# One TensorE order and one branch of a four-block transformer kernel: merge products exchanged, rotation buffer, value turn and logits moved

## The reference, cut to what matters

```python
# block 1, per layer
merge_g = sigmoid(merge_r @ w_merge_up).reshape(b, s, 4, 1024)
for n in range(4):
    yb = branches[n] * silu(gate_z[:, :, n])
    merged = merged + merge_g[:, :, n] * (yb @ w_branch[n])
out = merged @ w_out

# block 2, per layer, branch A
q = axial_rope(rmsnorm(q_a, qn_a)); k = axial_rope(rmsnorm(k_a, kn_a))
p = softmax(q @ k.T * scale);  o_a = (p @ v) * silu(g_a)
```

## Time and profile before

| | |
|---|---|
| median of 3 runs | 1513.04 us (1512.2 to 1513.24) |
| profiled execution, its own time | 1514.28 us |
| its span | 1512.5 us |
| TensorE busy | 1418.9 us (94% of the span) |
| VectorE busy | 854.7 us (57%) |
| ScalarE busy | 729.5 us (48%) |
| GpSimd busy | 384.2 us (25%) |

### The profile page before, as it was taken

The page is one execution under the profiler, slowest core; times in us unless marked ns, Lnnn a source line. Parts: engine busy times, 40 slices in busy tenths (PEclk is TensorE's granted clock), DMA queues, the critical chain, the costliest instruction groups (busy, mean ns, idle before and its releaser), DMA issues.

```text
span 1512.5 us, 21589 instructions
## 1 busy us (share of the span) xinstructions
PE 1418.9 (94%) x8202; PEld 1101.7 (73%) x8202; DVE 854.7 (57%) x1553; ACT 729.5 (48%) x1557; POOL 384.2 (25%) x273
## 2 busy tenths in 40 slices
PE   7999999999989999999988889997999989988997
PEld 6767677778987677787778856665778856665776
DVE  3655436456662653455577665457656474457655
ACT  3555446555244554555554544435444544445443
POOL 2232122345131322123553111311112112310111
PEclk9999999999999999999999999998999999998999
DMA  6413451126242221112265413511323422511311
GB/s 225 112 30 88 109 136 43 51 68 227 87 154 61 53 84 57 56 46 63 91 216 162 118 52 63 118 57 49 97 65 94 116 70 55 92 60 46 101 61 57
DMA packets 195373, 135.76 MB, mean 90 GB/s; under 512 B 91590, under 2 KB 185414, under 8 KB 195270
## 3 DMA queue, kind: packets, MB, share of 16 engines
q1 hardware_dynamic: 191494, 120.22, 29.0%
q10 hardware_dynamic: 3776, 14.16, 2.5%
HBM read 122.03 MB, written 12.32 MB: 89 GB/s over the span
## 4 chain that ended last, share of the span: by engine, by line
PE 74%; DVE 12%; ACT 7%; issue 3%; DMA 2%; POOL 1%; SPq 1%; ACTq 0%; DVEq 0%; POOLq 0%
PE pb L1477 19%; PE pb L1479 17%; PE pb L1478 17%; PE pb L1560 6%; PE pb L1499 6%; PE pb L1538 5%; ACT prob L1616 2%; ACT tmp L1616 2%; ACT wh L1635 1%; DVE wl L1983 1%; DVE xl L1990 1%; DMA wr<-w_out 1%; DVE prob L2235 1%; PE pb L1522 1%; PE pb L1510 1%
## 5 line engine op out<-in xcount | busy, mean ns | idle before, releaser
L2376 POOL TENSOR_TENSOR wl<-wr,wh 128x512 fp32r<-128x512 f32 x178 | 254.2, 1428 | 857.6 <-ACT wh L1635 853.6
L1477 PE MATMUL pb<-xh,wl 128*128 128x512 f32 (+1 forms) x880 | 356.1, 405 | 11.4 <-DVE xl L1990 8.5
L1479 PE MATMUL pb<-xh,wh 128*128 128x512 f32 (+1 forms) x880 | 327.7, 372 | 0.0
L1478 PE MATMUL pb<-xl,wh 128*128 128x512 f32 (+1 forms) x880 | 327.6, 372 | 0.0
L1983 DVE TENSOR_TENSOR wl<-wr,wh 128x512 fp32r<-128x512 f32 x208 | 169.5, 816 | 183.5 <-ACT wh L1635 183.2
L1635 ACT CAST wh<-wr 128x512 fp32r<-128x512 f32 (+1 forms) x386 | 218.9, 604 | 38.0 <-PE pb L1479 17.1
L1477 PEld LDWEIGHTS pb<-xh,wl 128*128 128x128 f32 x880 | 169.2, 192 | 82.3 <-issue 47.0
L1479 PEld LDWEIGHTS pb<-xh,wh 128*128 128x128 f32 x880 | 168.7, 192 | 29.9
L1478 PEld LDWEIGHTS pb<-xl,wh 128*128 128x128 f32 x880 | 169.6, 193 | 22.3 <-issue 3.6
L1477 PE MATMUL pb<-wh,xl 128*128 128x256 f32 x448 | 133.2, 297 | 16.5 <-DVE wl L1983 8.4
L1616 ACT ACTIVATE prob<-prob,small 128x512 f32<-128x512 f32 (+3 forms) x128 | 76.3, 597 | 138.6 <-DVE small L2198 138.5
(11 more groups left out here) (197 smaller groups left out, 2443.1 us busy)
## 6 DMA issues: line engine op xcount, KB each, us to landing
wr<-w_in SPq DMA_DIRECT2D x39, 1024.0 KB, 5.2
wr<-w_out SPq DMA_DIRECT2D x14, 1024.0 KB, 5.4
wr<-w_in SPq DMA_DIRECT2D x48, 256.0 KB, 4.6
wr<-w_branch SPq DMA_DIRECT2D x48, 128.0 KB, 2.3
x<-prob SPq DMA_DIRECT2D x12, 512.0 KB, 3.3
wr<-w_out SPq DMA_DIRECT2D x48, 128.0 KB, 3.0
wr<-w_mem_kv SPq DMA_DIRECT2D x4, 1024.0 KB, 5.5
prob<-x ACTq DMA_DIRECT2D x2, 2048.0 KB, 10.6
```

The source lines that it names most:

```text
L1477: e.matmul(ps, ll, rh, start=start, stop=False)
L1478: e.matmul(ps, lh, rl, start=False, stop=False)
L1479: t = e.matmul(ps, lh, rh, start=False, stop=stop)
L2376: t = e.tensor_tensor(wl[:, j % 2, c0:c1], wr[:, j % 2, c0:c1], wh[:, j % 2, c0:c1].bitcast(F32), ALU.subtract)
```

## The change

There are four edits. (1) In the first column tile of the merge, the first term's branch product is made ahead of its gate product. (2) In branch A the rotated part is written to `tmpz`, a scratch row, in place of a `TM` slot. (3) In branch A the values are turned later: not in `project`, but as a part of branch B's projection, behind its third fill step; for A, B and D the wait for the turned values goes from the logits to the product with the values. (4) In branch A, a block's logits come at least 5000 planned ns behind those of the block before.

```diff
+FRONTS = 5000
@@ attention
-        before, late = None, None
+        before, late, apart = None, None, 0
...
             for i in range(4):
+                if now() < apart:
+                    yield apart
                 es, mid, after = front(l, br, c, i, sm.get(c), rt)
                 ready = now() + EXPS.get(br, 4000)
+                if br == "A":
+                    apart = now() + FRONTS
                 yield 0
@@ merge_term
+        opening = m == 0 and first
+        if opening:
+            held = yield from gemm("br", w, c0, c0 + 128, ("y", l, n), (k0, k0 + 1))
         b = yield from gemm("up", w, c0, c0 + 128, ("mr", l), (k0 + 2,))
...
-        b = yield from gemm("br", w, c0, c0 + 128, ("y", l, n), (k0, k0 + 1))
+        b = held if opening else (yield from gemm("br", w, c0, c0 + 128, ("y", l, n), (k0, k0 + 1)))
@@ project, behind
-            b, t2 = GR[0].take(), TM.take()
+            b, t2 = GR[0].take(), None if br == "A" else TM.take()
             put("rope2", l=l, br=br, n=n, src=tm, b=b, tm=t2)
-            give(b, t2)
+            give(b, *[t2] * (br != "A"))
@@ project, end
-        b = GR[0].take()
-        put("vturn", l=l, br=br, b=b, tm=tm)
-        give(b, tm)
-        yield
+        def turned():
+            b = GR[0].take()
+            put("vturn", l=l, br=br, b=b, tm=tm)
+            give(b, tm)
+
+        if br == "A":
+            box["vturn"] = turned
+        else:
+            turned()
+            yield
+
+    def then_turned(fill, turned):
+        for n, x in enumerate(fill):
+            if n == 2:
+                turned()
+            yield x
@@ block 2
+            if br == "A":
+                fill = then_turned(fill, turned)
@@ heads_ready
             elif br in PAIRED:
                 w.wait_ge(v_fn, v_fn.at(("paired", l, br, 2)))
-                w.wait_ge(v_copy, v_copy.at(("vturn", l, br)))
@@ pv on TensorE
+                if br in PAIRED:
+                    w.wait_ge(v_copy, v_copy.at(("vturn", l, br)))
@@ rope2 on VectorE
-                src, t2 = tm(s["src"]), tm(s["tm"])
+                src, t2 = tm(s["src"]), tmpz[:, :] if br == "A" else tm(s["tm"])
...
+                if br == "A":
+                    w.wait_ge(v_fn, v_fn.at(("rotated", l, n - 1) if n else ("rms2", 2 + l, 3)))
```

More of the change, by code:

```diff
@@ L1104, in plan @@
         for n, br in enumerate("ABDC"):
-            u = box["u"]
+            u, turned = box["u"], box.get("vturn")
             box = {}
             fill = project(l, "ABDC"[n + 1], box) if br != "C" else out_partial(l, tail, box)
+            if br == "A":
+                fill = then_turned(fill, turned)
             if br == "B":
@@ L2284, in vector_program @@
                 w.wait_ge(aux, aux.at(b))
-                for g, v in s["tm"].free():
-                    w.wait_ge(g, v)
+                if br == "A":
+                    w.wait_ge(v_fn, v_fn.at(("rotated", l, n - 1) if n else ("rms2", 2 + l, 3)))
+                else:
+                    for g, v in s["tm"].free():
+                        w.wait_ge(g, v)
                 w.wait_ge(d_tab, d_tab.at((l, br)))
@@ L2294, in vector_program @@
                     w.wait_ge(heado, heado.at(("heado", l, "A", 1)))
-                ends = (s["tm"],) if br == "A" else (s["tm"], s["src"])
                 t = e.tensor_tensor(dst, src, t2, ALU.add)
-                t.then_inc(v_fn.sem, v_fn.mark(*([] if br == "A" else [("paired", l, br, n)]), ends=ends))
+                if br == "A":
+                    t.then_inc(v_fn.sem, v_fn.mark(("rotated", l, n)))
+                else:
+                    t.then_inc(v_fn.sem, v_fn.mark(("paired", l, br, n), ends=(s["tm"], s["src"])))
             elif k == "qnormed":
```

## The result

The changed kernel takes 1517.76 us (median of 11 runs, 1513.09 to 1519.53); the kernel before, in as many runs, 1513.04 (1512.1 to 1517.44). The ratio is 1.0022, with a 95% interval of 1.0012 to 1.0032: 1.8 to 4.8 us slower (the two medians lie 4.7 apart). The forecast was 1515.7 and slower by 2.7; its range holds the time, and the interval holds the 2.7. The profiled executions stand at spans of 1516.0 and 1512.5.

What follows compares the result with a forecast made beforehand. TensorE carries most of the chain, so time counts only where it idles. Openings 0, branch A 1.9 and 0, clock 2.0, behind the logits -1.2: 2.7 us more, 1515.7 as a median against 1513.04; range 1508.0 to 1519.5.

Steps and rivals of the forecast that it cites:

- Merge openings: Block 1's merge, both layers: TensorE's wait for the low half becomes 1.6 us for the tanh; 0.0 us each.
- The table load's price: Merge opening, ScalarE: load takes 1.28 us by its row; the skill's drain would end each opening 1.3 us later.
- Rival 3: Merge openings: the table load holds the tanh 1.28 us longer, 2.6 us on top, 1518.3; chance 0.03.
- Branch A, layer 0, up to the logits: Block 2: banks held behind VectorE's stretch bring logits at 892.2 against 890.95, one group left undone; 1.9 us lost.
- The wait of 1.4 for that bank: Branch A, layer 0: TensorE waits 1.4 us for VectorE's normalisation to free the squares' bank ahead of the value turn.
- Branch A, layer 1, up to the logits: Logits wait for the keys alone, 0.7 us earlier, with 0.69 left undone; 0.0, bounds 0.5 either way.
- The wait of 3.3 in one piece: Branch A, layer 1: TensorE stands about 3.3 us in one wait ahead of the logits.
- The clock: Branch A: 3.4 us at 0.50 behind long waits costs 1.7 us in layer 1, 0.3 in layer 0; 2.0 lost.
- Rival 2: Branch A, both layers: the lower clock lasts longer, as the 5.7 us seen elsewhere; 1519.3 us; chance 0.20.
- full clock throughout branch A: Sign that the forecast is wrong: no stretch at a clock of 0.5 in branch A.
- Behind the logits: Branch A: spacing removes waits of 1.36 and 0.25 us, new ones of 0.95 and 0.5 come; 0.6 gained per layer.
- Rival 1: Bubbles are filled: merges give 1.57 us each, spacing 1.6 each, no slow stretch; about -5 us, 1508; chance 0.22.

Runs made afterwards that it cites:

- e1: The kernel before with edit 1 alone (branch product ahead of gate product in the merge); ratio to the kernel before 1.0004.
- e6: The changed kernel with the table set that has the tanh chosen at branch fox's first logits, so no load in the merge opening; ratio to the kernel before 1.0007.
- e11: The kernel before with no table load in the merge opening and its order kept; ratio to the kernel before 0.9994.
- e5: The changed kernel with the third tile's rotation and squares in banks of the attention's ring; ratio to the kernel before 1.0010.
- e2: The kernel before with edit 2 alone (rotated part in the scratch row); ratio to the kernel before 1.0008.
- e7: e5's kernel with 3500 more planned ns of fill ahead of branch A's first logits; ratio to the kernel before 0.9929.
- e3: The kernel before with edit 4 alone (branch A's logits at a distance); ratio to the kernel before 0.9994.
- e9: The kernel before with only 3500 more planned ns of fill ahead of branch A's first logits; ratio to the kernel before 1.0003.
- e4: The changed kernel without edit 3 (values turned in A's own projection, waited for ahead of the logits); ratio to the kernel before 1.0018.
- e10: The changed kernel with e7's extra fill ahead of branch A's first logits but its own banks; ratio to the kernel before 0.9988.
- e12: e8's kernel with the distance between branch A's logits set to zero; ratio to the kernel before 0.9958.
- e8: e6 and e7 together; ratio to the kernel before 0.9904, median 1502.51 us.

## Why the prediction was right

The mechanism came as forecast: VectorE's stretch sets the logits of branch A, the table load sets the openings, and the loss is a longer wait with a slow stretch behind it. The sum was 2.7; the four places measure 2.59. That they agree so closely is luck, since the terms below miss by up to half a microsecond each way. The chances were less sure than the sum: 0.42 for a change within 0.2% and 0.36 for slower; the ratio came out at 0.22%.

- **Merge openings:** 0.0 each, measured +0.07 and +0.08. The tanh was to end at 281.95 and the branch product to start at 282.0; it is at 282.02 on the clock of before. e1 and e6 show the reason to be the table load behind the exponentials, and e11 that the load alone was not in the way before.
- **The table load's price:** the tanh starts 1.29 after the load's start, and with the load gone (e6) the opening is 1.4 shorter. The drain of about 1.38 that the Trainium skill ("ScalarE: Activation LUTs", What ACT_TABLE_LOAD costs) adds is not in these rows. Rival 3 falls.
- **Branch A, layer 0, up to the logits:** 1.9 lost. Two meetings with GpSimd were counted, and two are in the rows (1.22 and 1.66, together 1.5 over, not 2.0). Release was put at 886.2 and logits at 892.2, or 892.5 with the 0.3 of the clock; less the 0.30 by which this execution runs late they are at 885.9 and 892.24. The meetings came ahead of the third tile and none behind it, so VectorE freed the squares' bank when it did before (889.2), not at 889.7; the forecast's 889.7 also doesn't follow from "one fewer behind", which by 1.0 a meeting gives 890.2. The wait of 1.4 for that bank is not in the rows: the three groups ahead of it took 3.74 us at the lower level, not 2.1, and left 0.15. e5 shows that the bank is not the loss by itself: VectorE's stretch is.
- **Branch A, layer 1, up to the logits:** 0.0, measured 0.3 better (less the 3.00 by which this execution runs late ahead of the place, the logits are at 1224.40, 1.02 sooner, with 0.69 left undone). The wait of 3.3 in one piece came as 0.95 and 3.05.
- **The clock:** 2.0 lost. A stretch of 3.4 us came behind each long wait, where it was forecast. Rival 2's longer stretches did not come in this trace's branch A; in e6, with the same order there, one of 6.8 us did (883.7 to 890.5, partly under the wait), and the place cost 1.87, not 1.59. The forecast named only the wait of 1.88 us in layer 1, after which the clock stayed at full level, and left out the one of 1.94 in layer 0, after which it fell; "full clock throughout branch A" was thus no good sign for layer 0. That these stretches belong to the waits rests on e2, e5 and e7 (they move with the wait, and go with it); no run tested the clock apart from the waits.
- **Behind the logits:** 0.6 gained per layer. The places less the terms above leave 0.4 in layer 0 and, with 1.6 to 1.7 for the slow stretch, 0.4 to 0.5 in layer 1; the spacing alone gained 0.92 and 0.68 (e3). The wait at the reciprocals was put at 0.95 and is 0.73; the one ahead of branch B's value turn grew from 0.68 to 1.02, not by 0.5. Why the spacing gives less here than in e3 is open.
- **Rival 1** took the waits of rows 2 for losses of their own. e2 removed two of them and lost 2.2 us, e1 the other two and gained nothing. Of its terms only the spacing is real: 1.6 each were named, e3 gained 0.92 and 0.68.

The median lies 2.1 over the forecast. The places don't explain that. The two traces differ by 0.97 elsewhere; where the rest of the medians' difference arises was not traced, and the interval of 1.8 to 4.8 reaches down past the 2.7.

## What to carry to other kernels

A wait on the busiest engine is worth removing only if the engine that ends the chain behind it gets done sooner, or if there is work to put in its place: this change gathered VectorE's slack into one long wait and lost twice, by the wait and by the clock behind it, and the same buffer with free banks and five more groups of fill ahead of the logits turned +2.4 into -9.6 us at branch A. Ask of every edit which other one it needs (exchange and table load; buffer, bank and lead): exchange, load, buffer and lead each measured nothing or a loss alone. When an effect is a thousandth of the time, compare the traces place by place: the kernel before had medians of 1513.0, 1514.8, 1516.7 and 1515.5 us in the four sets of runs.

## What the runs showed of the hardware

Two loads of `w_out`, issued in one group in front of the output of block 1, landed after 12.08 us in the changed kernel and after 14.34 in e11, with the same order of instructions. Timeline of SyncE after, and of SyncE, ScalarE and TensorE in e11:

```profile
761.94 12.08 SPq L2470 DMA_DIRECT2D wr<-w_out  x2
```

```profile
762.88 14.34 SPq L2443 DMA_DIRECT2D wr<-w_out  x2
...
769.76 1.14 ACT L1637 CAST wh<-wr 128x512 fp32r<-128x512 f32 x2 [2.21 <-DMA wr<-w_out]
...
775.25 0.55 PE L1479 MATMUL pb<-wh,xl 128*128 128x256 f32 x1 [3.05 <-POOL wl L2378]
```

ScalarE's cast starts 2.21 us late, and TensorE then stands 3.05 for the low half. The shift of e11 grows by 3.2 us there, nearly all of its "elsewhere"; e5 has the same wait of 3.05 and the same 3.2. Why the loads landed later is open. The scatter of a transfer is thus as large as the change under study. The meeting of VectorE and GpSimd is the other: the same 128x512 cast took 1.24, 2.22 and 2.54 us in before, e5 and e9, by where GpSimd's additions, which follow transfers, happened to fall.

The clock: all eleven waits of 3.0 to 4.9 us that TensorE had ahead of branch A's logits or the gate product (changed kernel, e2, e4, e5, e6, and layer 0 of e10) had a slow stretch of 3.4 us behind them, or in e6's layer 0 one of 6.8 that began under the wait. Of the ten waits of 1.7 to 1.9 us for the third raw tile (before, e1, e3, e9, e11) three had one, all in layer 0 (before, e1, e9); the two of 2.3 us in e12 had none, nor had the waits of about 1 us in e7 and e8. Such a stretch costs an estimated 1.6 us where TensorE is the bound behind the wait (in the changed kernel's layer 0 its matmuls start 0.43 us apart in it and 0.23 outside), and nothing where another engine is, as in layer 0 of before.
